# Moving the weight copies of a bf16 block kernel to ScalarE's DMA queue, and unlinking the odd output-weight loads

## What is computed

```python
mod = silu(c) @ ada_w + ada_b                    # per sequence: shift, scale, gate
h = rmsnorm(x, norm_g) * (1 + scale) + shift
z = h @ w_in + b_in                              # 1024 -> 8192 columns
a_v, a_g, b_B, b_C, b_v, b_g, m_a, m_b = split(z)
y_a = group_linear(trailing_means(a_v) - a_v) * pool_scale * silu(a_g)
y_b = b_B * (causal_conv3(b_C * b_v) + conv_b) * silu(b_g)
merged = sigmoid(m_a) * (y_a @ w_out_a) + sigmoid(m_b) * (y_b @ w_out_b)
x = x + gate * (merged @ w_o)
out = rmsnorm(x, final_g)
```

## Time and profile before

| | us |
|---|---|
| median of 3 runs | 2577.73 |
| lowest and highest run | 2575.38, 2591.83 |
| the profiled execution, its own time | 2580.54 |
| span of its slowest core (core 0) | 2579.0 |
| span of its fastest core (core 5) | 2564.4 |
| PE busy, core 0 | 2475.3 (96%) |
| DVE, ACT, POOL busy, core 0 | 1295.0, 738.5, 216.8 |

### The profile page before, as it was taken

How to read it: one execution, slowest core, us unless ns; L and a number is a source line. 1 busy time by engine, 2 the same in 40 slices (tenths; PEclk the granted TensorE clock), 3 DMA queues, 4 the chain that set the end, 5 groups by cost and what they waited for, 6 DMA issues and landing times.

```text
span 2579.0 us, 32628 instructions; the slowest of 8 cores (2564.4 to 2579.0 us)
## 1 busy us (share of the span) xinstructions
PE 2475.3 (96%) x11552; PEld 1122.0 (44%) x11552; DVE 1295.0 (50%) x1421; ACT 738.5 (29%) x795; POOL 216.8 (8%) x302
## 2 busy tenths in 40 slices
PE   5997489999999999999999999999999999999997
PEld 2443134444444444444444444444444444444443
DVE  5553134564346544556345653556435663456524
ACT  3223013332233322332233222333223332222212
POOL 2111122101100110001000010001000010000000
PEclk9998799999999999999999999999999999999999
DMA  9956666545723473234423455234532447223341
GB/s 243 177 100 143 151 135 143 163 131 166 193 83 114 143 212 103 86 127 155 159 95 94 147 172 164 86 107 144 174 108 85 131 128 203 94 71 114 107 143 66
DMA packets 145182, 345.69 MB, mean 134 GB/s; under 512 B 17656, under 2 KB 17784, under 8 KB 145024
## 3 DMA queue, kind: packets, MB, share of 16 engines
q1 hardware_dynamic: 117952, 284.01, 34.0%
q0 software_dynamic: 26640, 59.26, 12.4%
q10 hardware_dynamic: 432, 0.35, 0.0%
HBM read 329.36 MB, written 54.56 MB: 149 GB/s over the span
## 4 chain that ended last, share of the span: by engine, by line
PE 86%; DMA 10%; issue 1%; SPq 1%; POOL 1%; DVE 0%; ACT 0%; POOLq 0%; DVEq 0%; ACTq 0%
PE ps_z L387 77%; PE ps_z L865 8%; DMA wb<-sb_wsl 8%; SPq L440 1%; DMA sb_wo<-wo 1%; DMA sb_xn<-adaw 1%; POOL sb_wsl L322 1%; DMA sb_wsl<-ws 0%; PE ps_z L535 0%; SPq L427 0%; POOLq L119 0%; PE ps_z L588 0%; POOL sb_wo L644 0%; POOL sb_stat L418 0%; DVE sb_t L733 0%
## 5 line engine op out<-in xcount | busy, mean ns | idle before, releaser
L387 PE MATMUL ps_z<-sb_hT,sb_wsl 128*128 128x512 bf16 x8000 | 1765.4, 380 | 25.3 <-DMA sb_wsl<-ws 24.5
L387 PEld LDWEIGHTS ps_z<-sb_hT,sb_wsl 128*128 128x128 bf16 x8000 | 783.8, 98 | 977.2 <-issue 41.6
L830 DVE TENSOR_TENSOR sb_t<-ps_z,sb_t 128x1024 f32<-128x1024 f32 x64 | 78.3, 1224 | 371.9 <-ACT sb_t L827 361.9
L387 PE MATMUL ps_z<-sb_yb,sb_wsl 128*128 128x512 bf16 x1024 | 235.1, 383 | 22.1 <-DMA sb_wsl<-ws 22.1
L387 PE MATMUL ps_z<-sb_ya,sb_wsl 128*128 128x512 bf16 x1024 | 235.4, 384 | 13.2 <-DMA sb_wsl<-ws 13.2
L865 PE MATMUL ps_z<-sb_wo,sb_mg 128*128 128x512 bf16 x1008 | 227.0, 379 | 1.0 <-DVE sb_mg L838 1.0
L418 POOL TENSOR_TENSOR sb_nwt<-sb_nwt,sb_mhalf 128x1 f32<-128x1 f32 x62 | 75.9, 1225 | 1786.4 <-DVE sb_nwt L415 1042.3
L719 DVE SCALAR_TENSOR_TENSOR sb_v<-ps_z,sb_cvec,sb_t 128x1024 f32<-128x1024 f32 x64 | 82.2, 1284 | 223.1 <-PE ps_z L387 220.8
L818 DVE TENSOR_TENSOR sb_t<-ps_z,sb_t 128x1024 f32<-128x1024 f32 x64 | 78.4, 1224 | 200.4 <-ACT sb_t L815 191.8
L827 ACT ACTIVATE sb_t<-ps_z,sb_cvec 128x1024 f32<-128x1024 f32 x64 | 71.2, 1113 | 368.9 <-PE ps_z L387 368.9
L387 PEld LDWEIGHTS ps_z<-sb_yb,sb_wsl 128*128 128x128 bf16 x1024 | 101.0, 99 | 146.1 <-issue 28.2
(11 more groups left out here) (117 smaller groups left out, 1399.8 us busy)
## 6 DMA issues: line engine op xcount, KB each, us to landing
sb_wsl<-wb SPq DMA_DIRECT2D x528, 256.0 KB, 2.8
sb_xn<-x SPq DMA_DIRECT2D x64, 512.0 KB, 5.8
y<-sb_xn SPq DMA_DIRECT2D x60, 512.0 KB, 3.0
sb_xt<-x SPq DMA_DIRECT2D x56, 512.0 KB, 4.7
sb_xf<-xT SPq DMA_DIRECT2D x56, 512.0 KB, 4.9
sb_wsl<-ws POOLq DMA_DIRECT2D x104, 256.0 KB, 5.1
wb<-sb_wsl POOLq DMA_DIRECT2D x72, 256.0 KB, 4.9
sb_wo<-wo POOLq DMA_DIRECT2D x32, 256.0 KB, 6.2
```

The costliest lines, as they stand in the source:

```text
L387: ins = e.matmul(Z[zb][:, sblk * 512:(sblk + 1) * 512], w[:, k, :], src[:, k, sblk * 512:(sblk + 1) * 512], start=(k == 0), stop=(k == 7))
L830: P.op("dve", lambda e: e.tensor_tensor(out=t2[:], in0=Z[zob][:], in1=t2[:], op=ALU.mult), reads=[bZ[zob], bT2[ti]], writes=[bT2[ti]])
```

## The change

Two lines. The copies from a weight slot to `wb` are issued by ScalarE, on its own DMA queue, at the same place of the program; GpSimd's list no longer holds them. And of the eight output-weight loads only the even ones are marked as writing `badg`, the gate's input: an odd one depends on nothing but earlier uses of its own part of `wo` (and stands behind its even neighbour in GpSimd's list).

```diff
@@ keep_w, L336
-            P.dma("pool", "k%d" % slot,
+            P.dma("act", "k%d" % slot,
                   lambda e: e.dma_start(out=wb_d[at], in_=wsl[slot][:].rearrange("p k n -> p (k n)")),
                   reads=[bws[slot]], writes=[bwb[at]])
@@ load_wo, dma_k, L643
                 P.dma("pool", "swo%d" % k,
                       lambda e: e.dma_start(out=wo[:, k, :], in_=wo_d[:, k * 1024:(k + 1) * 1024]),
-                      writes=[bwo[k], badg[k // 2]])
+                      writes=[bwo[k]] + ([badg[k // 2]] if k % 2 == 0 else []))
```

## The result

The changed kernel is faster: 0.971 of the kernel before, 95% interval 0.965 to 0.976. The profiled execution took 2505.99 us, another 2507.02 us; the forecast was 2510 us in a range of 2500 to 2542.

What follows compares the result with a forecast made beforehand. PE was taken as the bound, losing 76.3 us to late weights in pass 0: 2579.0 - 76.3 = 2502.7, plus 2.2 for core 4 and 1.5 outside the span, 2506.4; with 4 us of stalls 2510 us, range 2500 to 2542.

Steps and rivals of the forecast that it cites:

- The bound and the price of the stretch: From 188.42 to 406.36 us PE does 41 blocks in 217.9 us, undisturbed 141.6: 76.3 us lost to late weights.
- the allowance for remaining stalls: 4 us added to the forecast for stalls left in pass 0's crowded stretch, bounds 0 and 24.
- The mechanism of part 1: Copies on ScalarE free GpSimd's loads from waiting for copy landings, so pass 0's load rate becomes PE's.
- The latest case: In a merge step, block a's copy goes out some 6 us after block start, 2.6 after PE finished it.
- The share of part 1: Moving the copies to ScalarE was credited with the whole 76.3 us lost in pass 0.
- Part 2 at 0, bounds 0 to 5: Freeing odd output-weight loads removes four GpSimd waits, 20.0 us in pass 0, but gains 0 beside the copies' move.
- the lead of 24 us: Seven blocks x 3.45 us, 24.2 us, that copy and load may take before PE needs the weights.
- What is late next: Power operation for the next pass at 224 us, spreading some 10 us, VectorE wanting it about 237: barely in time.
- The DMA engines: In pass 0's shortened stretch the traffic needs 118 of 136 us, 87%; it fits with little to spare.
- Rival B: DMA engines become the bound in pass 0's stretch, 24 us more than the floor: 2530 us; chance 0.20.
- rival C: GpSimd keeps waiting for late copies; only 14 us of issuing and 20.0 us of output-weight waits saved: 2546 us; chance 0.06.
- rival D: ScalarE becomes the late engine, 72 copies at 1.57 us fully exposed, 113 us: 2619 us; chance 0.04.

Runs made afterwards that it cites:

- e8: e1 with pass 1's root of the frame norms taken by ScalarE and VectorE instead of GpSimd's power operation; 2510.0 us, 0.972.
- e9: e3 plus the change's dropped waits of odd output-weight loads for their even neighbours; 2506.2 us, 0.971.
- e3: Kernel before, copies still issued by GpSimd but each placed three blocks earlier in its list; 2515.1 us, 0.974.
- e7: Changed kernel with the copies in SyncE's list instead of ScalarE's; 2506.6 us, 0.971.
- e1: Changed kernel with odd output-weight loads again waiting for their even neighbours, so only the copies' move to ScalarE; 2522.8 us, 0.977.
- e2: Kernel before with only the odd output-weight loads freed of waiting for their even neighbours, copies on GpSimd; 2570.4 us, 0.9955.
- e5: Changed kernel with each slot copied a second time by ScalarE, to a spare DRAM tensor nobody reads; 2524.5 us, 0.979.
- e6: Changed kernel with four further 8 KB DMAs behind every copy in ScalarE's list; 2514.4 us, 0.975.
- e11: Changed kernel with one further 8 KB DMA behind every copy in ScalarE's list; 2506.0 us, 0.971.

## Why the prediction was right, and where it wasn't

**The bound and the price of the stretch: right.** 76.3 us of loss in 41 blocks, all given back; the last core at 2504.3 (forecast 2504.9 before stalls). That it was core 4 is chance: in the other execution core 1 was last, and core 4's gate starts at 177.87 us here, at 174.34 in e8 and at 178.67 in e9. The 4 us between 2510 and 2506 are the allowance for remaining stalls, of which the stretch had none.

**The mechanism of part 1: right, and shown.** Not the queue, not the issuing and not the traffic, but a load standing directly behind the copy it waits for. e9 undoes it without leaving GpSimd and reaches the changed kernel's time; e3, without part 2, wins 67 us, more than part 1 on ScalarE's queue; e7 reaches the same time from SyncE. The latest case, the copy of a merge step's block a, came out as worked out: for the block that ends at 255.7 us it is issued at 257.74, 2.0 us later (forecast 2.6). The Trainium skill ("DMA: Bandwidth & Descriptors", "Issuing engines are not separate DMA queues") says that DMAs from all issuing engines run on the same 16 DMA engines. The trace agrees: three queues share them at 48.5, 32.8 and 12.1%. The same section of the Trainium skill says that issuing from several engines saves only the issue time. By that, part 1 would be worth 26 x 0.55 = 14 us in the stretch; it was worth 60 (e1), because a wait for a landing was taken out of a list, and e3 shows that no second engine is needed for it.

**The share of part 1: too large.** The sum gives it all 76.3 us. Alone it won 60. The total came out because the bound, a PE that never waits, was right, and part 2 supplied what part 1 left: two errors of one size that cancel.

**Part 2 at 0, bounds 0 to 5: wrong.** It measured 16 us on top of part 1 (e1) and 12 us alone (e2). The step that failed is "each 5 us delay fits into the lead of 24 us". The delays were not 5 us: landings slow down when PE speeds up, and the four waits grew from 20.0 to 33.9 us. And "The power operation stands behind ScalarE's sums of squares, not behind copies" overlooked that it stands behind the output-weight loads in the same list, and that delay, 16 us in e1, doesn't pass through the lead of the weights at all. It took most of the 16 us (e8).

**What is late next: the place was right, the time short.** The power operation came at 225 us as worked out (224). But its two transfers took 6.9 us to the second issue and 10.5 to the landing, 17 in place of 10, and VectorE waited 4.5 us. "Barely in time" turned into slightly late, covered by PSUM as said on core 4, and nearly so on core 3 (1.3 us). The same chain, 16 us later, is what costs PE most in e1.

**The DMA engines: share 0.94 against my 0.87.** Loads and copies cost about what I took: the loads' queue used 48.5% of 142 us, 69 us, for some 41 loads at 1.7 us each (1.6 taken), and the 24 copies 17 us, 0.72 each (0.78 taken). The term that was too small is SyncE's traffic: 32.8% of 142 us, 47 us, for 12.85 MB, which at my rate of 0.334 MB per us makes 38; I had 37 in the sum. Rival B was closer than 0.20 suggests: e5 puts the edge at no more than one further copy per block.

**Signs that were set wrongly.** I wrote that no wait for a copy would exceed about 10 us, and that long waits for copies would speak for rival C. They are up to 15 us in pass 0 and 21.9 later, and PE doesn't notice. What counts is whether the next load still lands in its 24 us, not the wait in front of it, most of which can be time in which the block itself isn't done. ScalarE waited too, 19.7 us in four waits put down to landings of copies (half of the sign for rival D), and PE never waited for ScalarE in this stretch. Rival C's time, 2546 us, is excluded by the interval; rival D's by e6 and e11.

## What to carry to other kernels

In an in-order list, look for an instruction that waits for the landing of what the same list has just issued: put some rounds between the two (three blocks earlier did it here), or give one of them to another list; which engine hardly matters. Then walk the same list again for what else stands behind such waits, above all a small operation on the path of the next stage, because it is the next to be late. And price a wait by the landing times of the faster kernel, whose DMA is more crowded, not by those of the slow one.

## What the runs showed of the hardware that I had not expected

A full-looking DMA share is compatible with an undisturbed PE: 0.94 over 142 us with no wait of PE on core 4. From 210 to 230 us it even reads 1.06, so 1 isn't a ceiling of this figure. The median landing of a 256 KB load rose from 5.2 to 9.1 us, of the copy from 5.1 to 8.1, and a 4 KB store took 6.9 us until its follower could be issued. ScalarE's issues of the copy (duration ns min/median/max) were cheaper than its own late DMA in the earlier trace rows:

```profile
L337 ACTq DMA_DIRECT2D wb<-sb_wsl x72: 326/327/799, 112.0 to 633.4; - x72
```

SyncE's and ScalarE's copies are equally good for the time (2506.6 and 2506.5 us), and so are GpSimd's in e9 (2506.2). They aren't the same for the engines: a copy is 144 packets on ScalarE's queue and was 80 on GpSimd's, and from 188 to 330 us it lands after 8.1 us by the median on the one and after 10.3 on the other (e9).
